# Gate products with a stride of four floats in PSUM, runs of four in the evacuation, and one unit's weighted rows in eight on ScalarE

## What is computed

```python
# hf: (512, 1024); expert_down, expert_up: (128*128, 1024)
s1, s2 = scores of the token against 128 first and 128 second keys, for 8 heads
v1, i1 = top_k(s1, 16);  v2, i2 = top_k(s2, 16)
top_s, pos = top_k(v1[:, None] + v2[None, :], 16)      # 16 pairs (i1, i2) a head
gates = softmax(top_s)                                 # 128 slots a token
out[t] = sum over slots of gates * gelu(hf[t] . expert_down[i1*128 + i2]) * expert_up[i1*128 + i2]
```

## Time and profile before

| | us |
|---|---|
| median of three runs | 2797.38 (2790.15 to 2800.26) |
| the profiled execution, its own time | 2797.25 |
| its span in the profile | 2795.6 |
| PE, DVE, ACT, POOL busy | 2662.6, 1805.1, 943.1, 829.2 |

### The profile page before, as it was taken

One profiled execution on the slowest core, in us unless ns is written; L12 is line 12 of the kernel. 1 busy time (PEld: TensorE's weight loads), 2 busy tenths in 40 slices (PEclk: granted clock), 3 DMA queues, 4 the chain that ended last, 5 costly groups with the idle time before them and its releaser, 6 DMA issues.

```text
span 2795.6 us, 35889 instructions
## 1 busy us (share of the span) xinstructions
PE 2662.6 (95%) x12743; PEld 2118.7 (76%) x12743; DVE 1805.1 (65%) x3276; ACT 943.1 (34%) x1219; POOL 829.2 (30%) x530
## 2 busy tenths in 40 slices
PE   5999989999999999999999999999999999899997
PEld 3455445599877789999999887699877877688875
DVE  6842766699999688888888898550118533560532
ACT  2323223333477333233322222453233233332321
POOL 2100001155300134444444322244222243244442
PEclk7999999999999999999999999999999999999998
DMA  8511334333355799999999888223624432122321
GB/s 343 181 57 61 110 122 168 128 124 120 101 199 195 271 333 336 331 336 333 337 334 337 300 303 309 100 83 114 107 80 154 150 113 90 60 98 91 98 90 60
DMA packets 194874, 507.16 MB, mean 181 GB/s; under 512 B 31312, under 2 KB 83552, under 8 KB 192720
## 3 DMA queue, kind: packets, MB, share of 16 engines
q1 hardware_dynamic: 146608, 326.99, 35.7%
q0 software_dynamic: 48160, 178.87, 17.7%
HBM read 456.58 MB, written 49.22 MB: 181 GB/s over the span
## 4 chain that ended last, share of the span: by engine, by line
PE 63%; issue 16%; DVE 12%; POOL 5%; DMA 1%; ACT 1%; DVEq 1%; SPq 0%; POOLq 0%; ACTq 0%
PE psum L1681 19%; PE psum L1983 14%; PE psum L1668 13%; PE psum L547 6%; PE psum L562 6%; POOL l_r L890 5%; DVE arena L2053 3%; DVE arena L2050 2%; DVE look_oh L2050 2%; DVE arena L2057 1%; PE psum L1407 1%; PE psum L1990 1%; DVEq L2053 1%; DVE arena L2402 1%; DVE arena L2403 1%
## 5 line engine op out<-in xcount | busy, mean ns | idle before, releaser
L915 ACT ACTIVATE arena<-psum 128x512 f32<-128x512 f32 (+8 forms) x474 | 320.6, 687 | 1106.8 <-PE psum L1668 345.6
L2050 DVE TENSOR_TENSOR arena<-arena 128x384 f32<-128x384 f32 (+8 forms) x399 | 307.8, 777 | 493.2 <-ACT arena L915 265.7
L1681 PE MATMUL psum<-e_r,e_r 128*128 128x512 f32 x2304 | 541.1, 393 | 7.0 <-DVE e_r L2050 7.0
L890 POOL TENSOR_TENSOR l_r<-arena,l_r 128x1024 fp32r<-128x1024 f32 x144 | 351.1, 2439 | 655.3 <-ACT l_r L500 655.3
L1668 PE MATMUL psum<-e_r,e_r 128*128 128x384 f32 x2048 | 532.4, 340 | 4.5 <-ACT arena L915 2.4
L1681 PEld LDWEIGHTS psum<-e_r,e_r 128*128 128x128 f32 x2304 | 434.5, 189 | 96.2 <-issue 4.6
L915 ACT ACTIVATE e_r<-arena 128x1024 fp32r<-128x1024 f32 x256 | 270.3, 1057 | 367.9 <-PE psum L1681 346.6
L1668 PEld LDWEIGHTS psum<-e_r,e_r 128*128 128x128 f32 x2048 | 364.4, 188 | 15.5 <-POOL l_r L860 6.3
L1668 PE MATMUL psum<-e_r,l_r 128*128 128x384 f32 x1024 | 343.8, 336 | 0.0
L874 POOL DMA_INDIRECT arena<-in_down_rows,arena x128 | 160.3, 1253 | 431.4 <-DMA scratch_early<-arena 192.9
L874 POOL DMA_INDIRECT arena<-in_up,arena x128 | 162.1, 1266 | 247.8 <-DVE arena L2539 122.1
(11 more groups left out here) (230 smaller groups left out, 3321.3 us busy)
## 6 DMA issues: line engine op xcount, KB each, us to landing
arena<-in_down SPq DMA_DIRECT2D x128, 512.0 KB, 4.9
arena<-in_up SPq DMA_DIRECT2D x128, 512.0 KB, 6.7
scratch_gates<-arena SPq DMA_DIRECT2D x12, 2048.0 KB, 7.3
arena<-scratch_gates SPq DMA_DIRECT2D x30, 768.0 KB, 10.0
arena<-in_w_in SPq DMA_DIRECT2D x44, 512.0 KB, 3.6
arena<-in_w_ada POOLq DMA_DIRECT2D x40, 512.0 KB, 6.0
arena<-in_w_query SPq DMA_DIRECT2D x16, 512.0 KB, 3.5
arena<-in_w_glu SPq DMA_DIRECT2D x16, 512.0 KB, 3.6
```

Source lines behind the costliest of these rows:

```text
L890: nc.gpsimd.tensor_tensor(rr(lo, 1024, "l"), reg(RING + q % NSLOT * SLOT, 1024), rr(hi, 1024, "l").bitcast(F32), ALU.subtract).then_inc(S[ ...
L915: do(sc.activation(out, in_, f, **kw), sem)
L1681: last = mm(bank(2 * tt_ + hf), rr(w__ + tt_ * P, P), rr(x__ + hf * 512, 512), start=(first and n == 0), stop=(final and n == 2))
L2050: do(v.tensor_tensor(out, a, b, op), sem)
```

## The change

It has four parts.

1. Each gate product writes its 128 columns four floats apart in PSUM (token t at offset t), so that the four tokens of a unit stand side by side. ACT reads the bank in order and writes runs of four floats, the runs 32 floats apart. What arrives in the staging buffer is the same as before. ACT no longer waits for its own evacuation.
2. In unit 7 of every round DVE writes only the one-hot rows of i1. The four weighted rows come from ACT, into a buffer in `small`: one in each of the four turns of ACT's loop, as Relu(g - g * |i2 - iota|), that is an Abs of 128x128 at the head of the turn, and a Relu of 128x128 after the evacuation of the turn's first unit. PE waits for the fourth Relu (b_hotx) before the products of unit 7.
3. DVE's second four units of a round are written out with fixed addresses where they stood in a loop.
4. Before the first round ACT writes the negated gates of the units 7 (128x48) to `small`; a scratch area of a later stage, `mag8`, moves.

```diff
+        OBX = 96
+        minus_g = small[:, 608:656]
...
+            wait("slots_T", 3)
+            act_(minus_g.rearrange("p (c t) -> p c t", c=NGC),
+                 reg(GT, TD).rearrange("p (c x t) -> p c x t", c=NGC, x=8)[:, :, 7, :], ACT.Copy, scale=-1.0)
...
-                stg = reg(STG[c % 2], GCHUNK * P).rearrange("p (j t) -> p t j", j=P)
-                with tn.loop(8 // GB, g_evac=GB) as i:
+                stg = reg(STG[c % 2], GCHUNK * P).rearrange("p (j t) -> p j t", j=P)
+                with tn.loop(8 // GB, g_evac=GB, act_own=1, b_hotx=1) as i:
+                    hot = small[:, bass.ds(i * P + OBX, P)]
+                    act_(hot, con("iota"), ACT.Abs, "~act_own", scale=-1.0, bias=A[:, bass.ds(i + (I2T + 32 * c + 28), 1)])
                     for u_ in range(GB):
                         wait("g_mm", i * GB + (GB + c * 8 + u_ + 1))
-                        act_(stg[:, bass.ds(i * (4 * GB) + 4 * u_, 4), :],
-                             bank(u_).rearrange("p (t j) -> p t j", t=4), ACT.Copy, "g_evac")
+                        act_(stg[:, :, bass.ds(i * (4 * GB) + 4 * u_, 4)],
+                             bank(u_).rearrange("p (j t) -> p j t", t=4), ACT.Copy, "~g_evac")
+                        if u_ == 0:
+                            tn.settle("act_own")
+                            act_(hot, hot, ACT.Relu, "~b_hotx", scale=small[:, bass.ds(i + (608 + 4 * c), 1)],
+                                 bias=A[:, bass.ds(i + (GT + 32 * c + 28), 1)])
                 if c == NGC - 1:
+                    wait("g_evac", GB + TD // 4)
...
+                    if x % 8 == 7:
+                        pe.wait_ge(S["b_hotx"], S.base("b_hotx") + i * (4 * NSLOT) + 4 * (r + 1))
                     for t in range(4):
-                        last = mm(bank(u_)[:, t * P:(t + 1) * P], reg(OA + u_ * 512 + t * P, P),
-                                  reg(OB + u_ * 512 + t * P, P), start=True, stop=True)
+                        last = mm(bank(u_).rearrange("p (j t) -> p t j", t=4)[:, t, :], reg(OA + u_ * 512 + t * P, P),
+                                  small[:, OBX + t * P:OBX + (t + 1) * P] if x % 8 == 7 else reg(OB + u_ * 512 + t * P, P),
+                                  start=True, stop=True)
...
+                else:
+                    for n in range(4 * c, 4 * c + 4):
+                        u_ = n % GB
+                        wait("g_mm", n + 1)
                         tt(three(OA + u_ * 512, 4, P), bc(con("iota").unsqueeze(1), [P, 4, P]),
+                           bc(reg(I1T + 4 * n, 4).unsqueeze(2), [P, 4, P]), ALU.is_equal,
+                           "~b_hot" if n % 8 == 7 else FREE)
+                        if n % 8 < 7:
+                            for t in range(4):
+                                ts(reg(OB + u_ * 512 + t * P, P), con("iota"), reg(I2T + 4 * n + t, 1),
+                                   reg(GT + 4 * n + t, 1), ALU.is_equal, ALU.mult, "~b_hot" if t == 3 else FREE)
```

More of the change, by code:

```diff
@@ L139 @@
                    ("gq", 4), ("ff_split", 32)],
-    "act_6": [("u_hi", 128), ("l_hi", 144)],
+    "act_6": [("b_hotx", 48), ("u_hi", 128), ("l_hi", 144)],
     "pool_1": [("l_lo", 144)],
@@ L204, in wait, with settle @@
         self.eng.wait_ge(self.sems[sem], self.sems.base(sem) + value)
+    def settle(self, sem):
+        if self.i is None:
+            self.eng.wait_ge(self.sems[sem], self.sems.base(sem) + self.base[sem])
+        else:
+            self.eng.wait_ge(self.sems[sem], self.i * self.per[sem] + (self.sems.base(sem) + self.base.get(sem, 0) + self.k[sem]))
     @contextmanager
@@ L422, in build @@
         dtx, dt_t, dt_2, dt_s = (small[:, 464 + 64 * n:528 + 64 * n] for n in range(4))
-        mag8 = small[:, 256:320]
+        mag8 = small[:, 32:96]
         g_sq, g_mid = gsc[:, 8:16], mod[:, 0:8]
@@ L2490, in _ @@
             for c in range(2 * NGC):
[L2491 to L2494, removed]
-                        tt(three(OA + u_ * 512, 4, P), bc(con("iota").unsqueeze(1), [P, 4, P]),
[L2496 to L2500, removed]
+                if c % 2 == 0:
+                    with tn.loop(4 // GB, b_hot=GB) as i:
+                        for u_ in range(GB):
+                            n = 4 * c + u_
+                            wait("g_mm", i * GB + (n + 1))
+                            tt(three(OA + u_ * 512, 4, P), bc(con("iota").unsqueeze(1), [P, 4, P]),
+                               bc(A[:, bass.ds(i * (4 * GB) + (I1T + 4 * n), 4)].unsqueeze(2), [P, 4, P]), ALU.is_equal, FREE)
+                            for t in range(4):
+                                ts(reg(OB + u_ * 512 + t * P, P), con("iota"),
+                                   A[:, bass.ds(i * (4 * GB) + (I2T + 4 * n + t), 1)],
+                                   A[:, bass.ds(i * (4 * GB) + (GT + 4 * n + t), 1)], ALU.is_equal, ALU.mult,
+                                   "~b_hot" if t == 3 else FREE)
+                else:
+                    for n in range(4 * c, 4 * c + 4):
+                        u_ = n % GB
+                        wait("g_mm", n + 1)
+                        tt(three(OA + u_ * 512, 4, P), bc(con("iota").unsqueeze(1), [P, 4, P]),
+                           bc(reg(I1T + 4 * n, 4).unsqueeze(2), [P, 4, P]), ALU.is_equal,
+                           "~b_hot" if n % 8 == 7 else FREE)
+                        if n % 8 < 7:
+                            for t in range(4):
+                                ts(reg(OB + u_ * 512 + t * P, P), con("iota"), reg(I2T + 4 * n + t, 1),
+                                   reg(GT + 4 * n + t, 1), ALU.is_equal, ALU.mult, "~b_hot" if t == 3 else FREE)
```

## The result

The change makes the kernel slightly slower: 2798.49 us in the median of 15 runs against 2793.31 for the kernel before, measured beside it. The ratio is 1.0023, with a 95% interval of 1.0013 to 1.0034, that is 3.6 to 9.5 us, with 6.4 at the ratio itself. The forecast was 7.1 us. The absolute forecast, 2804.5, was counted from the median of three runs, 2797.38; the median of 15 lies 4.1 us lower, which is most of the 6.0 between 2804.5 and 2798.49.

The account below looks back on a forecast made before the run. PE bounds the kernel, DVE the changed stage. Eleven passages x 0.57 = 6.3 us, plus 0.76 behind the last round's unit 7, make +7.1 on 2797.38: 2804.5 us, range 2788 to 2826.

Parts of the forecast that it names:

- 0.19 us of slack: DVE's next unit 0 starts at 1.50; its buffers, freed by unit 6's products, allow 1.31.
- The chain in front of unit 7: Unit 6's products, evacuation, Relu, unit 7's products: unit 7 begins at 2.39 for 1.63, DVE's unit 1 0.57 late.
- E: Length of ACT's evacuation of a unit from PSUM to SBUF: 1.083 us before, taken as 0.60 after.
- ACT to PE: Time from the Relu's end on ACT to PE's start of unit 7: 0.11 us.
- PE's new wait: PE's unit 7 products wait for ACT once a round, about 0.96 us after PE is free.
- DVE's two waits: DVE's TENSOR_TENSOR waits for PE about 0.84 and 0.76 us at each passage from one round to the next.
- rival A: Strided PSUM writes hold PE: products doubled by 0.89 us a unit, 64 us slower, 2861; chance 0.2.
- the half rate of FP32 products: FP32 products deliver columns at half PE's contiguous PSUM write rate, so a write twice as dear might be hidden.
- B: Rival: the wait is hidden and DVE gains 12 x 0.19 = 2.3 us, 2795; chance 0.08.
- C: Rival: fixed addresses make DVE quicker, 3 x 0.20 us a round; with the 0.57 lost, 2797; chance 0.09.
- D: Rival: runs of four make the evacuation no cheaper, E = 1.08, 2810; chance 0.1.
- the low half: The low half of an expert matrix, once a round behind unit 3 on DVE: 1.12 us.

Follow-up runs that it names:

- relu_early: The change with the Relu directly behind its Abs, ahead of the wait for the products; 14.01 us a round, ratio 1.0001 to the kernel before.
- unroll_only: The kernel before with only DVE's second four units of a round written out with fixed addresses; 14.15 us a round, ratio 0.9996.
- rows_only: The change with products and evacuation as before, so only unit 7's rows move to ACT; 15.04 us a round, ratio 1.0061 to the kernel before.
- relu_first: The change with the Relu behind the wait for unit 6's products but ahead of its evacuation; 14.35 us a round, ratio 1.0001 to the kernel before.

## Why the prediction was right

**What bounds the stage.** Right. DVE was the bound, with 0.19 us of slack at the next round's unit 0; relu_early shows that unit at 1.32 where 1.31 was worked out. Its gain is 0.15 and not 0.19, because the round I read is not all rounds: in every fourth round of the kernel before (unit 6 at 761.08, 817.73 and 874.37) DVE's units 0 and 1 stand at 1.43 and 3.06 and not at 1.50 and 3.13. The means over the eleven passages are 1.48 and 3.11.

**The chain in front of unit 7.** Right in its terms but one: evacuation at 1.30 (1.30 forecast), E 0.597 (0.60), the next instruction 0.50 later (0.50), Relu 0.486 (0.48). Off was ACT to PE, 0.05 for 0.11. The row I took it from names DVE as the releaser of the weight load; PE there waits for DVE and for an evacuation, one after the other, and its sequencer has a step of 0.05 us for the second wait (L1702) right before the load. That this is the difference was not tried. So unit 7 began at 2.33 for 2.39, and DVE's unit 1 was at 3.64, 0.51 late for 0.57 by the passage quoted. Against the mean of before, 3.11, it is 0.53, and DVE's next step is 1.64 for 1.63: that makes the 0.54 of the rounds. The sum becomes 11 x 0.54 + 0.70 = 6.7, and the measured interval is 3.6 to 9.5.

**What agreed by luck, and what was a little off.** PE's new wait was forecast at 0.96 and is 0.97, but as 2.33 less 1.36 and not 2.39 less 1.43: back to back PE takes the next unit after 1.36 us (782.75 to 784.11). In the passage of before from which I had 1.43, the weight load of the next unit starts 0.06 after the one ahead of it ends (797.42 to 797.48). Nothing hung on it, as DVE's unit 2 had no further wait either way. DVE's two waits were forecast at 0.84 and 0.76 and are 0.78 and 0.60: I counted both from where the next instruction would have started, 0.07 before the last one ends, and unit 7 came 0.06 earlier.

**The strided products, rival A.** Nothing, as taken: a unit's products take 0.89 us before and after (780.42 to 781.31). The Trainium skill's sentence in Advanced Engine Details and Errata, Memory Cachelines, that any non-contiguous PSUM pattern significantly slows matmuls, does not hold for these FP32 products at a stride of four floats. Whether the half rate of FP32 products is the reason, as I argued, was not tried. The same section's rule for SBUF, full speed for accesses that stay on a line of 16 bytes, agrees: runs of four floats take 0.597 us for 512 elements, as contiguous ones do (0.598), and single floats 1.083.

**The other rivals.** B (the wait is hidden) needed the Relu ahead of unit 7; relu_early built that case and got the small gain it named in the rounds (0.15 for 0.19), though the whole time doesn't show it. C (fixed addresses) fell with unroll_only, D (the evacuation as dear as before) with the evacuation's row, 597 ns.

**What I did not see** while predicting is the use of my own reading: a row of the kernel before that shows PE waiting 1.40 us for DVE behind the low half, and so the place where a dropped instruction counts in full:

```profile
786.08 0.97 PEld L1704 LDWEIGHTS psum<-arena 128*128 128x128 f32 x8 [1.40 <-DVE arena L2053]
```

## What to carry over

Taking work off the engine that bounds a stage pays only where its next instruction is not about to wait: before moving work, look at how much slack the buffer wait behind it has (here 0.19 us of 1.03, of which 0.15 was gained), and pick the step at which the consumers are already waiting (behind the low half, where the same move gave all of it). And work that is handed to an idle engine must be placed by when it is needed: one Relu, moved ahead of the wait for the products with the same instructions on every engine, was worth 0.70 us a round.

## What the runs showed of the hardware

- From the end of PE's products to the start of the ACT instruction that waits for them 0.13 us pass for an evacuation (one wait) and 0.24 for a Relu with a second wait and two operands at addresses from registers (relu_first). The sequencer's steps lie open there; behind a running evacuation they cost nothing (the change).
- ACT's next instruction starts 0.10 us before a contiguous evacuation ends (0.60 long, 0.50 apart) but 0.21 us before a strided one ends (1.05 long, 0.84 apart in rows_only; 1.08 and 0.87 in the mean of its 48).
- FP32 products of 128 columns write PSUM with a stride of four floats at the same pace as side by side (275 ns the median record, 0.89 us for four products, with and without the stride).
